# Two width-4 convolutions as products with diagonals on TensorE, and the wide convolution on VectorE alone, in a two-layer decoder step

## What is computed

```python
u = h @ p['w_in'][l]
xa, ga, xb, zb, xc, gc = jnp.split(u, SPLITS, axis=-1)
a = xa * jax.nn.sigmoid(ga)
a, new_buf_a = causal_dwconv(a, buf_a, p['conv_a_w'][l], p['conv_a_b'][l])      # width 31, 256 channels
a_out = jax.nn.silu(group_layernorm(a, p['ln_a_g'][l], p['ln_a_b'][l], G_A))
cb, new_buf_b = causal_dwconv(xb, buf_b, p['conv_b_w'][l], p['conv_b_b'][l])    # width 4, 512 channels
cb = jax.nn.silu(cb)
q = headwise(cb, p['w_q'][l])
k = headwise(cb, p['w_k'][l]) * (DH_B ** -0.5)
v = headwise(xb, p['w_v'][l])
...
xcv, new_buf_c = causal_dwconv(xc, buf_c, p['conv_c_w'][l], p['conv_c_b'][l])   # width 4, 256 channels
hc, hc1 = rglru(xcv, hc0.astype(f32), p['w_ra'][l], p['b_ra'][l], p['w_ix'][l], p['b_ix'][l], p['lam'][l])
```

## Time and profile before

| | |
|---|---|
| runs | median 1021.25 us of 3 (1020.48 to 1021.67) |
| profiled execution | 1018.2 us; its span, first to last instruction, 1016.4 us |
| busy | PE 895.7 us (88%), DVE 764.1 (75%), ACT 544.9 (54%), POOL 179.8 (18%) |
| chain that ended last | PE 72%, DVE 22%, ACT 3%, issue 2%, DMA 1% |
| layer 0's mixers | some 45 to 195 us |
| layer 1's mixers | some 413 to 560 us |

### The profile page before, as it was taken

One profiled execution on the slowest core, in us unless ns is written; L12 is line 12 of the kernel. 1 busy time (PEld: TensorE's weight loads), 2 busy tenths in 40 slices (PEclk: granted clock), 3 DMA queues, 4 the chain that ended last, 5 costly groups with the idle time before them and its releaser, 6 DMA issues.

```text
span 1016.4 us, 14109 instructions
## 1 busy us (share of the span) xinstructions
PE 895.7 (88%) x5300; PEld 780.7 (77%) x5300; DVE 764.1 (75%) x957; ACT 544.9 (54%) x547; POOL 179.8 (18%) x229
## 2 busy tenths in 40 slices
PE   4968786899999999978789699999999999999970
PEld 3966655899999999957568578787888788888850
DVE  3599987555665545799976678888888888888856
ACT  5424741434443335346503377777777777777750
POOL 1299132400000001693412200000000000000001
PEclk9988777899999999998879789999999999999995
DMA  9480204797545656821133369999999999999933
GB/s 315 123 256 1 83 11 126 289 416 258 200 127 181 213 180 223 241 80 43 51 99 113 147 249 332 383 361 381 363 379 347 394 354 384 358 387 351 389 125 126
DMA packets 116605, 239.85 MB, mean 236 GB/s; under 512 B 12756, under 2 KB 35046, under 8 KB 116541
## 3 DMA queue, kind: packets, MB, share of 16 engines
q1 hardware_dynamic: 107069, 206.75, 57.7%
q0 software_dynamic: 8048, 27.16, 7.7%
q10 hardware_dynamic: 1440, 5.28, 1.3%
HBM read 213.70 MB, written 26.04 MB: 236 GB/s over the span
## 4 chain that ended last, share of the span: by engine, by line
PE 72%; DVE 22%; ACT 3%; issue 2%; DMA 1%; POOL 0%; POOLq 0%; DVEq 0%; ACTq 0%
PE ps L544 10%; PE ps L545 9%; PE ps L546 9%; PE ps L806 8%; PE ps L808 8%; PE ps L807 8%; DVE low L315 3%; PE ps L820 3%; PE ps L822 3%; PE ps L821 3%; DVE ac L1253 3%; DVE cb L1253 2%; PE ps L664 1%; ACT whi L1098 1%; DVE Cs L1494 1%
## 5 line engine op out<-in xcount | busy, mean ns | idle before, releaser
L315 DVE TENSOR_TENSOR low<-raw,whi 128x2048 fp32r<-128x2048 f32 (+2 forms) x204 | 434.1, 2135 | 105.3 <-ACT whi L1098 58.9
L1098 ACT ACTIVATE whi<-raw 128x2048 fp32r<-128x2048 f32 (+1 forms) x144 | 254.9, 1775 | 85.4 <-PE ps L808 38.0
L544 PE MATMUL ps<-nhi,whi 128*128 128x264 f32 x736 | 215.9, 293 | 11.2 <-DVE low L315 6.3
L545 PE MATMUL ps<-nlo,whi 128*128 128x264 f32 x736 | 213.4, 290 | 0.0
L546 PE MATMUL ps<-nhi,low 128*128 128x264 f32 x736 | 212.5, 289 | 0.0
L912 ACT ACTIVATE whi<-raw 128x2048 fp32r<-128x2048 f32 (+1 forms) x60 | 109.4, 1825 | 119.0 <-PE ps L546 119.0
L544 PEld LDWEIGHTS ps<-nhi,whi 128*128 128x128 f32 x736 | 143.5, 195 | 13.5 <-issue 12.0
L806 PE MATMUL ps<-whi,ehi 128*128 128x512 f32 (+1 forms) x384 | 147.0, 383 | 5.1 <-issue 3.5
L808 PE MATMUL ps<-whi,elo 128*128 128x512 f32 (+1 forms) x384 | 145.0, 378 | 0.0
L807 PE MATMUL ps<-low,ehi 128*128 128x512 f32 (+1 forms) x384 | 144.9, 377 | 0.0
L545 PEld LDWEIGHTS ps<-nlo,whi 128*128 128x128 f32 x736 | 143.3, 195 | 0.1
(11 more groups left out here) (376 smaller groups left out, 1270.0 us busy)
## 6 DMA issues: line engine op xcount, KB each, us to landing
raw<-in_we_down SPq DMA_DIRECT2D x40, 1024.0 KB, 6.6
raw<-in_we_gate SPq DMA_DIRECT2D x32, 1024.0 KB, 7.1
raw<-in_we_up SPq DMA_DIRECT2D x32, 1024.0 KB, 7.1
raw<-in_w_in SPq DMA_DIRECT2D x16, 1024.0 KB, 5.7
xs<-zero POOLq DMA_DIRECT2D x5, 2560.0 KB, 30.3
raw<-in_we_gate SPq DMA_DIRECT2D x16, 768.0 KB, 8.3
raw<-in_we_up SPq DMA_DIRECT2D x16, 768.0 KB, 6.5
raw<-in_w_gate SPq DMA_DIRECT2D x10, 1024.0 KB, 5.4
```

Source lines behind the costliest of these rows:

```text
L315: return engine.tensor_tensor(low[:, u % NRAW, part], raw[:, u % NRAW, part], whi[:, u % NHI, part].bitcast(F32), ALU.subtract)
L544: pe.matmul(o, hi[:, k, c], xhi[:, kx, :], start=first, stop=False)
L545: pe.matmul(o, hi[:, k, c], xlo[:, kx, :], start=False, stop=False)
L1098: act.activation(whi[:, c % NHI, 0:kt * w], raw[:, c % NRAW, 0:kt * w], ACT.Copy).then_inc(hi_done, 1)
```

## The change

In both layers the two width-4 convolutions leave VectorE. For each tap and plane a 128x128 diagonal of that tap's weights is built in `diag` (24 of them): the 16 of xb on VectorE, the 8 of xc on ScalarE. TensorE then multiplies: for a plane, one product over all 264 columns (the last tap, prompt and samples at once) and for each of the other three taps one over 256 prompt columns and one over the 8 sample states, all summed in one bank (`conv`). `conv_b` stands between the two units of group 2, in banks 4 to 7, and `conv_c` between the k and the v products. ScalarE adds the bias on the way out: Silu for `cb`, Identity for `xcv`. The v products go ahead of r and i. VectorE takes all 31 taps of the wide convolution, in parts that end at taps 18, 21, 26 and 31; its samples come right after `xbp`; `ix` moves behind part 1. GpSimd keeps neither taps nor the early ones of `v1`: it sets those once `xcv` is done, because `diag` lies where `ktok`, `v1` and `E` come later.

The gates' products wait for the last of `ix` and for `vT`, so here for everything in this list down to L1020. The diff, cut to its core:

```diff
-POOL_TAPS = 13
-DVE_TAPS = (POOL_TAPS, 20, 23, 27, 31)
+TAPS = (0, 18, 21, 26, 31)
...
+            def conv(b, i, weights, src, state):
+                o = bank(b + i, T)
+                pe.matmul(o, diag[:, weights + 3, :], src[:, i, 3:3 + T], start=True, stop=False)
+                for j in range(3):
+                    pe.matmul(o[:, 0:TP], diag[:, weights + j, :], src[:, i, j:j + TP], start=False, stop=False)
+                    last = pe.matmul(o[:, TP:T], diag[:, weights + j, :], state[:, j, :], start=False, stop=(j == 2))
+                return last
+            def conv_b(l):
+                pe.wait_ge(S["diag_b"], l + 1)
+                pe.wait_ge(free[1], HALF1[l])
+                for i in range(H):
+                    last = conv(4, i, 4 * i, xbp, B_(l, 7, i, 24).rearrange("p (b k) -> p k b", k=3))
+                last.then_inc(S["cb_ps"], 1)
+            def conv_c(l):
+                pe.wait_ge(S["diag_c"], l + 1)
+                pe.wait_ge(S["q_out"], l + 1)
+                for i in range(2):
+                    last = conv(4, i, 16 + 4 * i, xcp, C_(l, 16, i, 24).rearrange("p (b k) -> p k b", k=3))
+                last.then_inc(S["xcv_ps"], 1)
...
-                for g in range(3):
+                for g in range(2):
                     group(20 * l + g, nhi, nlo)
                     if l == 0 and g == 0:
                         parameter_turns()
+                group(20 * l + 2, nhi, nlo, (0,))
+                conv_b(l)
+                group(20 * l + 2, nhi, nlo, (1,))
                 mixers(l)
...
+                for i in range(2):
+                    for j in range(CC):
+                        last = act.activation(diag[:, 16 + 4 * i + j, :], ident[:, :], ACT.Copy, scale=C_(l, j, i))
+                last.then_inc(S["diag_c"], 1)
                 act.wait_ge(S["ga_in"], l + 1)
...
-                act.wait_ge(S["cb_conv"], l + 1)
-                act.activation(cb[:, :, :], cb[:, :, :], ACT.Silu).then_inc(S["cb_done"], 1)
+                act.wait_ge(S["cb_ps"], l + 1)
+                for i in range(H):
+                    last = act.activation(cb[:, i, :], bank(4 + i, T), ACT.Silu, bias=B_(l, 4, i))
+                last.then_inc(S["cb_done"], 1)
...
+            def conv_b_diagonals(l):
+                if l == 0:
+                    dve.wait_ge(S["start_dve"], 2)
+                else:
+                    dve.wait_ge(used, FIRST_UNIT[20])
+                for i in range(H):
+                    for j in range(CB):
+                        last = dve.tensor_scalar(diag[:, 4 * i + j, :], ident[:, :], B_(l, j, i), None, ALU.mult)
+                last.then_inc(S["diag_b"], 1)
...
                 step(dve.tensor_scalar(lam4(L[5]), lam, 0.0, None, ALU.min))
+                conv_b_diagonals(0)
                 dve.wait_ge(S["lam_exp"], 1)
...
                 dve.wait_ge(used, U + 2)
-                dve.wait_ge(S["pads"], 6 * (l + 1))
+                if l == 1:
+                    conv_b_diagonals(l)
+                dve.wait_ge(S["pads"], 5 * (l + 1))
...
                 conv_a_taps(1)
+                dve.wait_ge(S["xcv_done"], l + 1)
+                dve.wait_ge(S["ri_done"], 4 * (l + 1))
+                step(dve.tensor_tensor(ix[:, :, :], ix[:, :, :], xcv[:, :, :], ALU.mult))
                 dve.wait_ge(S["gate_ln"], l + 1)
...
-                dve.wait_ge(S["conv_a_taps"], 2 * (l + 1))
-                dve.tensor_tensor(ac[:, :, 0:TP], ac[:, :, 0:TP], pool_taps(vg), ALU.add).then_inc(S["conv_a_done"], 1)
...
-                pool.wait_ge(S["apad_done"], l + 1)
-                total, product = pool_taps(vg), pool_taps(Cp)
...
+                pool.wait_ge(S["xcv_done"], l + 1)
+                pool.memset(v1[:, :, :, P:P + 1], 1.0).then_inc(S["v1_ones"], 1)
                 pool.wait_ge(S["q_out"], l + 1)
```

More of the change, by code:

```diff
@@ L188, in build @@
         ix = sb("ix", [P, 2, T], where=mix)
+        with ExitStack() as early:
+            diag = sb("diag", [P, 24, P], where=early)
         ktok = sb("ktok", [P, 3, H * P], where=mix)
@@ L565, in mixer_products @@
                 last.then_inc(S["k_ps"], 1)
-                pe.wait_ge(S["q_out"], l + 1)
+                conv_c(l)
+                pe.wait_ge(S["k_out"], l + 1)
+                for h in range(H):
+                    last = pe.matmul(bank(h, T), wq[:, 2, h, :], xbp[:, h, 3:3 + T], start=True, stop=True)
+                last.then_inc(S["v_ps"], 1)
                 pe.wait_ge(S["xcv_done"], l + 1)
@@ L981, in layer @@
                 act.activation(kT[:, :, :], ps[:, 0:4, 0:T], ACT.Copy, scale=float(P) ** -0.5).then_inc(S["k_out"], 1)
+                act.wait_ge(S["xcv_ps"], l + 1)
+                for i in range(2):
+                    last = act.activation(xcv[:, i, :], bank(4 + i, T), ACT.Identity, bias=C_(l, 4, i))
+                last.then_inc(S["xcv_done"], 1)
+                act.wait_ge(S["v_ps"], l + 1)
+                act.activation(vT[:, :, :], ps[:, 0:4, 0:T], ACT.Copy).then_inc(S["v_out"], 1)
                 act.wait_ge(S["ri_ps"], l + 1)
@@ L1243, in scaled @@
                 return dve.tensor_tensor(dst, ps[:, b:b + planes, 0:T], rstd[:, :, :].to_broadcast([P, planes, T]), ALU.mult)
[L1245 to L1253, removed]
@@ L1344, in layer @@
                 scaled(xbp[:, :, 3:3 + T], 4, 4).then_inc(free[1], 1)
[L1345 to L1348, removed]
+                dve.wait_ge(S["apad_done"], l + 1)
+                samples_conv_a(l).then_inc(S["conv_a_done"], 1)
                 dve.wait_ge(used, U + 6)
@@ L1352, in layer @@
                 scaled(xcp[:, :, 3:3 + T], 0, 2).then_inc(free[0], 1)
[L1353 to L1357, removed]
-                lo(U + 6)
[L1359 to L1363, removed]
+                lo(U + 6)
                 tmp, sq = rg_temp(0), rg_temp(1)
-                dve.wait_ge(S["ri_done"], 4 * (l + 1))
-                step(dve.tensor_tensor(ix[:, :, :], ix[:, :, :], xcv[:, :, :], ALU.mult))
                 def conv_a_taps(part):
[L1371 to L1374, removed]
+                    first, end = TAPS[part:part + 2]
+                    for j in range(first, end):
+                        for i in range(2):
+                            if j == 0:
+                                step(dve.tensor_scalar(ac[:, i, 0:TP], apad[:, i, 0:TP], A_(l, 0, i), A_(l, 31, i), ALU.mult, ALU.add))
+                            else:
+                                settle(1 - i if j == CA - 1 else 1)
+                                ins = dve.scalar_tensor_tensor(ac[:, i, 0:TP], apad[:, i, j:j + TP], A_(l, j, i), ac[:, i, 0:TP], ALU.mult, ALU.add)
+                                if j < CA - 1:
+                                    step(ins)
+                                else:
+                                    ins.then_inc(S["conv_a_done"], 1)
                 conv_a_taps(0)
```

71 lines of the change are left out of this document (20 added, 51 removed).

## The result

The changed kernel takes **1024.91 us** (median of 20 runs, 1020.83 to 1026.90) against 1020.41 us before (20 runs, 1018.16 to 1022.06): ratio **1.0045**, 95% interval 1.0037 to 1.0053, so 4.6 us slower. The forecast was 1.25 us faster, within 0.2%, that is no change. The time lies in the range, on the side of rivals B and C, but it moved the other way.

The account below looks back on a forecast made before the run. Bound: a mixer's chain of TensorE, VectorE, ScalarE. Layer 0 wins 5.4 us, layer 1 loses 4.15: 1.25 won, so the profiled 1018.2 gives 1017.0; 3.05 more for the median makes 1020.0 us, range 1015.5 to 1025.5.

Parts of the forecast that it names:

- Rival B: TensorE's short products are bound by loading weights: 0.25 us each, 4.5 us more, 1024.5 us; chance 0.11.
- Rival C: TensorE's clock falls ahead of the gates: 6.8 us more, 1026.8 us in one layer, 1033.6 in both; chance 0.09.
- Its sum for layer 0: Gates at 86.3 us plus 32.95 to the second `lna` product: 119.25 against 124.64, 5.4 us won.
- 4.15 us of loss: Layer 1: gates at 458.3 us, second `lna` product at 491.25 against 487.09.
- the price of an 8-column product: TensorE's convolution products over the sample states: 0.125 us each, 18 a layer, 2.25 us.
- signs of being wrong: Layer 0 gains under 3 us; layer 1 loses under 2; part 0 outlasts the gates' row; 1.2 GHz after gap.
- The diagonals: The 16 on VectorE in layer 0: 0.2 us each, 3.2 us, some 0.1 staying on the path to group 1.
- From the start of the rows to the columns: VectorE's stretch behind the gates: 8.29 us plus 0.8 for two more taps in part 2, 9.1 us.
- from there to the second `lna` product: From the columns 11.07 us to the square of `ac`, set by ScalarE's list, then 0.68.
- Taps cost 0.40 us without GpSimd: VectorE's taps of 256 columns take 0.396 us with GpSimd idle, so its 26 more taps cost nothing.
- D: VectorE's taps stay at 0.63 us: part 0 takes 22.7 us, VectorE is the bound, about 1032 us; chance 0.02.
- the removal of `cb`'s wait: TensorE's standstill of 8.22 us in layer 0 behind group 2 goes, and TensorE runs without a hole.

Follow-up runs that it names:

- experiment 1: The changed kernel with the 8-column products of both convolutions left out: 1015.87 us, ratio 0.9958 to the kernel before.
- experiment 2: The changed kernel with each 8-column product made 64 columns wide: 1024.91 us, a single run read only for its trace.
- experiment 4: The changed kernel once more, no edit, for a second profile: 1025.80 us, a single run.
- experiment 5: Against the kernel before: width-4 convolutions stay on VectorE, GpSimd's taps go to VectorE as well: 1005.55 us, ratio 0.9853.
- experiment 7: The changed kernel with convolution samples on VectorE, nine taps moved into its wait for group 2, and filler products ahead of the gates: 1013.76 us, ratio 0.9933.
- experiment 3: The changed kernel with four extra 264-column products a layer in TensorE's hole ahead of the gates: 1021.41 us, ratio 1.0009.
- experiment 8: The kernel of experiment 5 with the prompt columns of `xcv` moved to TensorE and filler products ahead of the gates: 1002.47 us, ratio 0.9822.

## Why the prediction was wrong

Its sum for layer 0 put the second `lna` product at 119.25 us; it came at 122.58. Three terms make up the 3.33 us, and what else differs cancels: `conv_b` 9.56 against 8.45, `conv_c` 4.74 against 4.23 (77.18 to 81.92), and 7.15 against 5.43 for the gates: 1.11 + 0.51 + 1.72 = 3.34. For layer 1, 4.15 us of loss were forecast, and 4.15 + 3.34 = 7.49. It came to 4.65 us behind after starting some 2.96 ahead (`conv_b` starts at 427.28; less a unit of 5.82, group 2 starts at 421.46, before at 424.42): 7.6.

- **The step that failed: the price of an 8-column product.** I took 0.125 us from short products that follow each other; it is 0.22. 36 of them, 0.09 too cheap, are 3.3 us. I called that row the nearest ("same operands, same engine, back to back") and read its x2 as one product of two records. It is not: L478 and L480 are transposes, two in a row (the loops at L477 and L479), and each makes one record. Four more of them stand right behind, here with the loads of their weights (timeline of before, PEld):

```profile
37.83 0.32 PEld L483 LDWEIGHTS ps<-ident,rowsB 62*128 62x128 f32 x4
```

Their loads start 0.06 us apart ((0.32 - 0.14)/3, with 0.14 us for one), those of the diagonal products 0.11. So the row holds another kind of product, whose loads stand closer. In the change the start behind a short product comes after 0.14 us, near the forecast; the rest is paid in the wide product behind it, which the row could not show. The rule of the Trainium skill that I set aside ("TensorE: Matmul & The Clock Gate", "LDWEIGHTS (loading the stationary operand)") gives, as an estimate for two loads, 0.21 us and would have made the sum some 1023 us; experiments 1 and 2 agree with it. The 0.06 us of the transposes does not, and there the measurement decides: the rule was weighed against a row that did not test it.

- **Rival B came near by luck.** Its 0.25 us comes from transposes too (L470, eight in a row). At 0.22 it gives 1020.0 + 3.3 = 1023.3 us and not 1024.5. Forecast, short products and the clock's 1.7 us a run (experiment 4) come to -1.25 + 3.3 + 1.7 = 3.8 us slower, against 4.6 measured, 3.8 to 5.4 by the interval.
- **Rival C was real, and smaller.** The hole was 2.27 us, as forecast (2.4). The clock fell, but for some 3.3 us of products, so it cost 1.72 us in a layer and not 6.8, and not in every run. Given only 0.09, it deserved much more: the earlier trace rows held a fall after a hole of similar length, the trace before had one behind 2.70 us ahead of r and i (experiment 5), and the argument against it, long work ahead of the hole, did not hold. Two of the prediction's own signs of being wrong came true: layer 0 gained 2.06 us, less than 3, and a stretch after the gap ran at 1.2 GHz.
- **The two mistakes add up.** Taken out together they give 11 us (experiment 7), where the forecast's error in the median is 5.8: the mended kernel also stops paying the part of each short product that had been forecast.
- **What held.** The diagonals took 3.22 us (forecast 3.2), and nothing of it reached TensorE: group 2's first unit ended at 58.13 us, before at 58.16. TensorE has no hole from group 0 to r and i. From the start of the rows to the columns it is 9.08 us (forecast 9.1), from there to the second `lna` product 11.75 (forecast 11.75). Taps cost 0.40 us without GpSimd, so D is out, and the layers do differ in sign as forecast: layer 0 gains, layer 1 loses. One reading was off without harm: the earlier trace rows show VectorE's taps four times and not five.
- **What the prediction did not ask.** It saw that GpSimd's taps had slowed VectorE's, and still priced the removal of `cb`'s wait as a gain of the products. The wait's cause went away with the other part of the change: with that part alone it is 0.57 us (experiment 5). Measured against that kernel the products put 9.56 + 4.74 us a layer on TensorE's path, for holes of 2 us.

## What to carry to other kernels

When a change has two parts, ask of each wait which part alone would end it; here one part freed VectorE, and the other then moved onto TensorE's path what VectorE could have hidden. Price a short product by the start of the wide one behind it, since its change of weights may be paid there, and take the price from a row whose product is of the same kind and makes as many records. And on a path, keep the hole ahead of a run of products small: here four products that nobody needs, put into a wait, cost nothing and kept the clock up.

## What was not expected of the hardware

- Widening twelve products from 8 to 64 columns left `conv_b` at 9.56 us: between wide products a short one cost 0.22 us at either width.
- Two loads of 128 columns started 0.11 us apart behind a short FP32 product and 0.06 us apart in a row of transposes.
- The same hole of 2.27 us was followed by a granted clock of 0.50 in 5 of 10 cases, in the same kernel once in both layers and once in one. Holes of 1.23 us (before and experiment 5, both layers) and of 0.49 us (experiments 3, 7 and 8, both layers) ahead of the gates were not.
- A tap's time beside GpSimd was not a steady slowdown: it ran from 472 to 1664 ns, and was 475 to 479 once GpSimd's taps were gone.
